# A two-operation token shift, expert dots moved into earlier stages, five value batches a unit, and gathers listed by when their slots come free

## The chip, the cores and the metric

The kernel runs on one core of one Trainium2 chip, in float32. The metric is the device time of one execution in microseconds, the median of the runs. The core's engines are named as the profile names them: PE (TensorE matmuls), PEld (its weight loads), DVE (VectorE), ACT (ScalarE), POOL (GpSimd) and SP (SyncE), with 16 DMA engines beside them.

## The reference, cut to what matters

A first block of two layers works on 256 image tokens `x` and 256 context tokens `xc`; a second block of one hybrid layer follows (the change does not touch it). A layer of the first block has a token mixer and an expert part (PEER):

```
z = h @ w_in
zr = z + mu[0] * (z_previous - z) + mu[1] * (z_next - z)      # token_shift; zero outside
y_a = rwkv(zr)                       # two scans, 16 heads of 64, forward and backward
y_b = conv_branch(z)                 # gated 31-tap depthwise convolution
x = x + gate1 * ((gates_a * y_a + gates_b * y_b) @ w_out)

# peer: for each token, 8 heads x 16 chosen experts out of 16384, 1024 numbers each
act[t, k] = gelu(h[t] . u[eidx[t, k]]) * gw[t, k]
out[t] = sum_k act[t, k] * v[eidx[t, k]]
```

The expert part is applied to `xc` in layer 0, to `x` in layer 0 and to `x` in layer 1. In layer 1 the context tokens only feed the scan states.

## The kernel before, in words

**Stages.** The program is written out by hand as a sequence of stages (`k.stage()`), each with one instruction list for each engine, and a stage starts when the one before it is done. Inside a stage engines wait for one another through counting semaphores. A matrix product is `gemm`: blocks of 128 output channels, weights from a ring of four 512 KB slots that SP fills, PSUM banks 0 to 3 evacuated by ACT. With `shift` given, DVE then does the token shift of each block (lines 226 to 241): a difference of neighbours, two one-column operations for the edges and two scalar_tensor_tensor operations, five in all.

**One expert job.** 256 tokens x 128 experts are fetched as 256 *rows* and 64 *batches*. A row is one indirect DMA from `peer_u` (128 partitions x 4 KB = 512 KB, line 1729) and one *dot* on DVE (128 x 1024, line 1688); rows go through a ring of four slots. A batch is one small POOL copy (line 1745), four indirect DMAs from `peer_v` (line 1751), 512 KB each, into four free slots, and 8 matmuls over the 4 strips (line 1713). The first 32 batches open when 128 dots are done and weighed (`weigh_tile`), the other 32 when 256 dots are done and the first 32 are summed (`finish_tile`).

**Where a job is spread.** Three jobs exist. The context job of layer 0 is spread over the token mixer of `x` in layer 0 and its `choose_experts`; the token job of layer 0 over the context mixer of layer 1, and what is left is done alone in `finish_experts`; the job of layer 1 is done wholly alone. How much a stage takes is written by hand: `use_rows(k, dve, n)` puts n dots at that place of DVE's list, `use_batches(k, pe, n)` n batches at that place of PE's list. `fetch_rows(k, pool)` then writes the gathers for them into POOL's list, each behind a wait for its slot to come free; POOL issues strictly in that order. The slots of values are `spare_slots`: the four weight slots and three borrowed buffers while the eight RWKV units of layer 0 run (seven, so one batch whole and three quarters of the next), four and four buffers in layer 1 and four plus the four of the row ring in `choose_experts`.

**The RWKV unit.** `rwkv_unit` handles a quarter of the heads in one direction; there are eight in a mixer. PE and DVE pass small products back and forth: a start part (pair products), a 14-step inversion (`invert_pairs`, q = 0 to 13), and two scan steps (n = 0, 1). `fetch_rows` is called three times in a unit: after the start part, after the inversion, at the end. While values are open, a unit takes 20 dots (DVE) and 4 batches (PE: one at its start, two in step n = 0, one in step n = 1); while they are not, 27 dots (26 in layer 1).

**`choose_experts`.** PE runs 16 blocks of the query product with 8 batches among them, then the transposes of `h`, then all batches that are left (line 1984), and behind them the transposes of the chosen expert numbers, for which DVE's sort must be done (line 2034).

## Time and profile before

| | us |
|---|---|
| median of 3 runs (lowest, highest) | 5637.92 (5622.06, 5640.57) |
| the profiled execution, its own time | 5637.74 |
| its span | 5636.0 |
| PE busy | 3746.9 |
| DVE busy | 2625.6 |
| POOL busy | 1682.2 |

1.74 us of the profiled execution lie outside its span. All times below are microseconds from the span's start. In a timeline row the columns are start, length, engine, line, operation, output and inputs, count, and in brackets the idle time just before it with what ended it. A row may merge several neighbouring instructions (x16). The mean granted clock of PE was 0.817 over the span.

### The profile page before, as it was taken

What the parts mean: (1) busy time and instruction counts of PE and PEld (TensorE: products, weight loads), DVE (VectorE), ACT (ScalarE), POOL (GpSimd) and SP (SyncE); (2) the same over time, 40 slices, a digit from 0 to 9 for tenths busy, and PEclk for the clock granted to TensorE, in tenths of its full rate; (3) what the DMA queues carried; (4) which work ended last, traced back from release to release, by engine and by line L of the source; (5) the groups of instructions that cost most, each with busy time, mean ns of one, the idle gap of its engine ahead of it and who ended that gap; (6) DMA issues with size and microseconds to landing.
All of it is one profiled execution on the core that took longest, in us unless ns stands there. A gap on an engine that the chain in (4) does not pass through costs nothing. (4 is left out here: it accounts for less than half of the span.)

```text
span 5636.0 us, 92419 instructions
## 1 busy us (share of the span) xinstructions
PE 3746.9 (66%) x37266; PEld 2834.6 (50%) x37266; DVE 2625.6 (47%) x6231; ACT 994.2 (18%) x2532; POOL 1682.2 (30%) x1745
## 2 busy tenths in 40 slices
PE   7888875896666684866625688887400456555988
PEld 5677764785444451655401367776300013554877
DVE  3556536668665261687640024663899101233110
ACT  1123311113222010233300012431100000111110
POOL 0000000325556344355677300000277773000000
PEclk9899987997788885867868899998755788766999
DMA  6520034766778687577899633002499996100433
GB/s 264 189 90 3 3 112 172 291 250 192 238 267 282 238 298 263 185 236 256 282 390 409 244 109 101 3 3 79 150 389 405 405 409 246 60 17 31 142 114 125
DMA packets 299199, 1118.78 MB, mean 199 GB/s; under 512 B 33712, under 2 KB 39104, under 8 KB 290240
## 3 DMA queue, kind: packets, MB, share of 16 engines
q0 software_dynamic: 221184, 805.40, 39.1%
q1 hardware_dynamic: 77632, 307.95, 15.9%
q8 instruction: 279, 4.57, 0.3%
q14 instruction: 104, 0.85, 0.0%
HBM read 1112.18 MB, written 1.05 MB: 198 GB/s over the span
## 5 line engine op out<-in xcount | busy, mean ns | idle before, releaser
L1729 POOL DMA_INDIRECT ring<-in_peer_u,expert_number x617 | 712.9, 1155 | 1812.9 <-DVE expert_number L2026 1173.4
L159 PE MATMUL psum<-h,weight_ring 128*128 128x256 f32 x3904 | 871.9, 387 | 45.8 <-PEq L85 45.8
L1688 DVE CUSTOM_DVE_ANT_0 ring<-ring,tok 128x1024 f32<-128x1024 f32 x617 | 746.1, 1222 | 251.0 <-DMA ring<-in_peer_u,expert_number 227.6
L159 PEld LDWEIGHTS psum<-h,weight_ring 128*128 128x128 f32 x3904 | 759.3, 195 | 157.7 <-issue 48.1
L1713 PE MATMUL psum<-spare,picked 128*32 128x512 f32 x1856 | 322.3, 828 | 437.3 <-DMA spare<-in_peer_v,expert_turned 422.4
L1751 POOL DMA_INDIRECT spare<-in_peer_v,expert_turned x464 | 440.2, 949 | 124.5 <-issue 115.0
L1713 PEld LDWEIGHTS psum<-spare,picked 128*32 128x32 f32 x1856 | 69.9, 133 | 686.2 <-issue 686.2
L1870 DVE SCALAR_TENSOR_TENSOR x_tokens<-psum,gate,x_tokens 128x128 f32<-128x128 f32 x32 | 8.6, 343 | 608.3 <-PE psum L1859 608.3
L1961 PE MATMUL psum<-h,weight_ring 128*128 128x256 f32 x768 | 186.5, 399 | 44.0 <-DMA weight_ring<-in_w_q 29.3
L1377 PE MATMUL psum<-h,weight_ring 128*128 128x256 f32 x768 | 177.9, 394 | 28.2 <-PEq L85 23.6
L1688 DVE CUSTOM_DVE_ANT_0 spare<-spare,tok 128x1024 f32<-128x1024 f32 x151 | 185.0, 1225 | 21.4 <-DMA spare<-in_peer_u,expert_number 15.6
L1961 PEld LDWEIGHTS psum<-h,weight_ring 128*128 128x128 f32 x768 | 150.6, 201 | 73.9 <-DMA weight_ring<-in_w_q 30.2
L1377 PEld LDWEIGHTS psum<-h,weight_ring 128*128 128x128 f32 x768 | 151.4, 199 | 53.3 <-issue 26.3
L1090 POOL MEMSET W<- 128x1024 f32 x4 | 3.8, 953 | 579.5 <-POOLq L85 579.5
L2135 PE MATMUL psum<-constants,dots 128*128 128x128 f32 x3 | 1.4, 475 | 254.7 <-DVE dots L2107 254.7
L1729 POOL DMA_INDIRECT spare<-in_peer_u,expert_number x151 | 155.3, 1029 | 45.7 <-issue 45.7
L1713 PE MATMUL psum<-weight_ring,picked 128*32 128x512 f32 x332 | 84.4, 894 | 108.8 <-DMA weight_ring<-in_peer_v,expert_turned 108.8
L641 ACT ACTIVATE E<-psum 128x256 f32<-128x256 f32 x288 | 110.4, 383 | 259.0 <-PE psum L660 252.3
L1323 DVE SCALAR_TENSOR_TENSOR zc<-u,vec,zc 128x256 f32<-128x256 f32 x336 | 133.3, 479 | 0.0
L1850 ACT ACTIVATE y<-psum 128x512 f32<-128x512 f32 x12 | 6.5, 594 | 709.3 <-PEq L85 709.3
L2135 PEld LDWEIGHTS psum<-constants,dots 128*128 128x128 f32 x3 | 0.5, 183 | 256.9 <-DVE dots L2107 255.2
L185 ACT ACTIVATE z<-psum 128x256 f32 x132 | 50.6, 383 | 436.7 <-PE psum L159 436.7
(552 smaller groups left out, 7133.6 us busy)
## 6 DMA issues: line engine op xcount, KB each, us to landing
weight_ring<-in_w_in SPq DMA_DIRECT2D x228, 512.0 KB, 3.5
ada_ring<-in_ada_w SPq DMA_DIRECT2D x34, 1024.0 KB, 9.2
weight_ring<-in_w_q SPq DMA_DIRECT2D x48, 512.0 KB, 5.0
weight_ring<-in_w_out SPq DMA_DIRECT2D x32, 512.0 KB, 3.6
weight_ring<-in_w_gate SPq DMA_DIRECT2D x32, 512.0 KB, 3.7
weight_ring<-in_w_mlp_in SPq DMA_DIRECT2D x32, 512.0 KB, 3.5
weight_ring<-in_w_mlp_out SPq DMA_DIRECT2D x8, 2048.0 KB, 8.4
ring<-in_ada_w SPq DMA_DIRECT2D x14, 1024.0 KB, 14.7
```

The costliest lines, as they stand in the source:

```text
L159: mm = pe.matmul(k.bank(slot, tokens), ring[:, slot, j * P:j * P + P], rhs(j), start=(j == 0), stop=(j == w.kt - 1))
L185: ins = act.activation(out, product, ACT.Copy)
L641: act.activation(out[:, g], product(q, g), ACT.Copy).then_inc(k.act_step.up(), 1)
L1323: ins = dve.scalar_tensor_tensor(conv[:, j, :], src, w, conv[:, j, :], ALU.mult, ALU.add)
L1377: mm = pe.matmul(k.bank(slot, 256), k.ring[:, slot, j * P:j * P + P], rhs(j), start=(j == 0), stop=(j == 7))
L1688: dve.tensor_tensor_reduce(place.rows, place.rows, b.tok[:, tile, :], 1.0, 0.0, ALU.mult, ALU.add, b.dots[:, tile, slot:slot + 1]).then_in ...
L1713: mm = pe.matmul(out, place.window.columns[:, strip, STRIP - 1 - c:2 * STRIP - 1 - c], part.rows[:, 512 * half:512 * half + 512], start=(c ...
L1729: pool.indirect_dma_start(place.rows, None, b.tables["u"], bass.IndirectOffsetOnAxis(ap=b.number[:, r:r + 1], axis=0)).then_inc(place.sem, 16)
L1751: pool.indirect_dma_start(part.rows, None, b.tables["v"], bass.IndirectOffsetOnAxis(ap=job.lists.turned[:, token:token + 1], axis=0)).then ...
L1850: act.activation(b.y[:, 512 * half:512 * half + 512], k.bank(bank + half), ACT.Copy).then_inc(k.act_step.up(), 1)
L1870: dve.scalar_tensor_tensor(part, k.psum[:, P * j:P * j + P], job.lists.gate[:, j:j + 1], part, ALU.mult, ALU.add).then_inc(k.vec_step.up(), 1)
L1961: mm = pe.matmul(k.bank(slot, 256), k.ring[:, slot, j * P:j * P + P], h[:, j, :], start=(j == 0), stop=(j == 7))
```

## The change

1. **Token shift.** ACT writes each block twice: once unchanged into `unshifted`, once multiplied by `kept` = 1 - mu0 - mu1. DVE adds the two neighbours, two scalar_tensor_tensor operations a block. Two small operations ahead make `kept`, and ACT waits for them.
2. **Dots.** `channel_norm` takes 6 (before 4, or 2 when it centers), `gates_and_taps` 24 (16), the shifted `gemm` 1.5 per block (0.75), `key_norms` 3 and 5 (1 and 2).
3. **Batches.** A unit takes five: at its start, behind q = 3 and q = 8 of the inversion, and one in each scan step; the second one of n = 0 is gone.
4. **Gathers.** One `fetch_rows` a unit, at its end. Every use notes a step (`step_of`: 100 for each stage plus the place in it), slots and windows carry the step at which they came free, and the gathers of a stage are sorted by it, rows before batches at equal steps. Before, rows were dealt evenly between the batches.
5. **`value_slots`** lends the row ring to values only from the stage after the last dot.
6. **`choose_experts`**: the left batches stand behind the transposes of the expert numbers.

```diff
@@ -40,6 +40,7 @@
+        self.stages, self.step = 0, 0
@@ -82,8 +83,14 @@
+        self.stages += 1
+        self.step_of(0)
...
+    def step_of(self, n):
...
+        self.step = 100 * self.stages + n
@@ -121,7 +128,8 @@
-            steps = mem.enter_context(k.sbuf("token_steps", [2, tokens + 1]))
+            unshifted = mem.enter_context(k.sbuf("unshifted", [w.blocks, tokens]))
+            kept = mem.enter_context(k.sbuf("share_kept", [w.blocks]))
@@ -176,12 +184,17 @@
+                if shift is not None:
+                    act.wait_ge(k.vec_step.sem, k.vec_step.at(2))
...
-                        if sigmoid is None:
+                        if shift is not None:
+                            act.activation(unshifted[:, bass.ds(i * SLOTS_W + slot, 1), :], product, ACT.Copy)
+                            ins = act.activation(out, product, ACT.Copy, scale=kept[:, bass.ds(i * SLOTS_W + slot, 1)])
+                        elif sigmoid is None:
@@ -224,28 +237,25 @@
-                        block_n, e = i * SLOTS_W + slot, steps[:, slot % 2, :]
-                        z = dst[:, bass.ds(block_n, 1), :].rearrange("p n t -> p (n t)")
+                        block_n = bass.ds(i * SLOTS_W + slot, 1)
...
-                        dve.tensor_tensor(e[:, 1:tokens], dst[:, bass.ds(block_n, 1), 1:tokens].rearrange("p n t -> p (n t)"),
-                                          dst[:, bass.ds(block_n, 1), 0:tokens - 1].rearrange("p n t -> p (n t)"), ALU.subtract).then_inc(up.sem, 1)
-                        dve.tensor_copy(e[:, 0:1], dst[:, bass.ds(block_n, 1), 0:1].rearrange("p n t -> p (n t)")).then_inc(up.sem, 1)
-                        dve.tensor_scalar(e[:, tokens:tokens + 1], dst[:, bass.ds(block_n, 1), tokens - 1:tokens].rearrange("p n t -> p (n t)"),
-                                          -1.0, None, ALU.mult).then_inc(up.sem, 1)
-                        for n in range(2):
...
-                            dve.wait_ge(up.sem, i * (5 * SLOTS_W) + up.at(5 * slot + 3 + n))
-                            dve.scalar_tensor_tensor(z, e[:, n:n + tokens], shift[:, n, bass.ds(block_n, 1)], z, ALU.mult, ALU.subtract
-                                                     ).then_inc(up.sem, 1)
...
-                    use_rows(k, dve, 3 * w.blocks // 4)
+                        for n, (to, source) in enumerate(((slice(1, tokens), slice(0, tokens - 1)), (slice(0, tokens - 1), slice(1, tokens)))):
+                            if n:
...
+                                dve.wait_ge(up.sem, i * (2 * SLOTS_W) + up.at(2 + 2 * slot + n))
+                            z, neighbour = (t[:, block_n, part].rearrange("p n t -> p (n t)") for t, part in ((dst, to), (unshifted, source)))
+                            dve.scalar_tensor_tensor(z, neighbour, shift[:, n, block_n], z, ALU.mult, ALU.add).then_inc(up.sem, 1)
...
+                    dve.tensor_tensor(kept[:], shift[:, 0], shift[:, 1], ALU.add).then_inc(up.sem, 1)
+                    dve.wait_ge(up.sem, up.at(1))
+                    dve.tensor_scalar(kept[:], kept[:], -1.0, 1.0, ALU.mult, ALU.add).then_inc(up.sem, 1)
+                    use_rows(k, dve, 3 * w.blocks // 2)
...
-                k.vec_step.up(5 * w.blocks)
+                k.vec_step.up(2 + 2 * w.blocks)
@@ -394,7 +404,7 @@
             chain = chained(k, dve)
-            use_rows(k, dve, 2 if center else 4)
+            use_rows(k, dve, 6)
@@ -622,12 +632,9 @@
             unit.between(q, dve)
+            k.step_of(2 + q)
...
                 use_rows(k, dve, 1)
...
-    @block.gpsimd
-    def _(pool):
-        fetch_rows(k, pool)
@@ -659,6 +666,9 @@
+            if q in (3, 8):
+                k.step_of(2 + q)
+                use_batches(k, pe, 1)
@@ -829,6 +839,7 @@
+            k.step_of(0)
@@ -837,10 +848,12 @@
+            k.step_of(1)
...
+            k.step_of(0)
@@ -890,10 +903,6 @@
-        @block.gpsimd
-        def _(pool):
-            fetch_rows(k, pool)
@@ -939,6 +948,7 @@
+            k.step_of(17)
@@ -974,6 +984,7 @@
+                k.step_of(18 + 2 * n)
@@ -989,6 +1000,7 @@
+                k.step_of(22)
@@ -1030,6 +1042,7 @@
+                k.step_of(18 + 2 * n)
@@ -1053,8 +1066,6 @@
-                if n == 0:
-                    use_batches(k, pe, 1)
@@ -1126,14 +1137,14 @@
             chain(dve.reciprocal(norm, norm))
-            use_rows(k, dve, 1)
+            use_rows(k, dve, 3)
...
                 chain(dve.tensor_tensor(part, part, halves[n], ALU.mult))
-            use_rows(k, dve, 2)
+            use_rows(k, dve, 5)
@@ -1406,7 +1417,7 @@
                 conv_taps(k, L, u, conv, reach, taps, True)(dve)
-                use_rows(k, dve, 16)
+                use_rows(k, dve, 24)
@@ -1591,17 +1602,17 @@
-        self.freed, self.taken, self.left = None, False, 0
+        self.freed, self.taken, self.left, self.step = None, False, 0, 0
...
-        return names(rows=self.rows, sem=self.landed.sem, landed=self.landed.count, freed=self.freed, slot=self)
...
-    def leave(self, sem, value, order=0):
-        self.freed, self.taken, self.left = (sem, value), False, order
+        return names(rows=self.rows, sem=self.landed.sem, landed=self.landed.count, freed=self.freed, step=self.step, slot=self)
...
+    def leave(self, sem, value, step, order=0):
+        self.freed, self.taken, self.step, self.left = (sem, value), False, step, order
@@ -1609,7 +1620,7 @@
-        self.columns, self.freed = columns, None
+        self.columns, self.freed, self.step = columns, None, 0
@@ -1618,7 +1629,7 @@
-        self.row, self.fetched, self.places, self.turn = 0, 0, {}, 0
+        self.row, self.fetched, self.places, self.turn, self.stage = 0, 0, {}, 0, 0
@@ -1658,7 +1669,7 @@
-    slots = [*k.spare_slots, *(job.shared.slots[0:4] if job.row == 2 * SLOTS and not k.own_slots else [])]
+    slots = [*k.spare_slots, *(job.shared.slots[0:4] if job.row == 2 * SLOTS and job.stage < k.stages and not k.own_slots else [])]
@@ -1668,7 +1679,7 @@
-                              free=window.freed)
+                              free=window.freed, step=window.step)
@@ -1687,8 +1698,8 @@
-        place.slot.leave(k.row_used.sem, k.row_used.count)
-        job.row = r + 1
+        place.slot.leave(k.row_used.sem, k.row_used.count, k.step)
+        job.row, job.stage = r + 1, k.stages
@@ -1713,9 +1724,9 @@
-        place.window.freed = k.batch_used.sem, k.batch_used.count
+        place.window.freed, place.window.step = (k.batch_used.sem, k.batch_used.count), k.step
...
-            part.slot.leave(k.batch_used.sem, k.batch_used.count, k.batch_used.count)
+            part.slot.leave(k.batch_used.sem, k.batch_used.count, k.step, k.batch_used.count)
@@ -1763,15 +1774,13 @@
-    done = 0
-    for n, m in enumerate(batches):
-        upto = len(rows) * (n + 1) // (len(batches) + 1)
-        for r in rows[done:upto]:
-            gather_row(k, pool, r)
-        done = upto
-        gather_batch(k, pool, m)
-    for r in rows[done:]:
-        gather_row(k, pool, r)
+    wanted = [(place_row(job, r).step, 0, r, gather_row) for r in rows]
+    latest = 0
+    for m in batches:
+        latest = max(latest, place_batch(k, m).step, *(part.step for part in place_batch(k, m).parts))
+        wanted.append((latest, 1, m, gather_batch))
+    for _, _, n, gather in sorted(wanted, key=lambda w: w[:3]):
+        gather(k, pool, n)
@@ -1981,8 +1990,6 @@
-                use_batches(k, pe, 2 * BATCHES)
-                k.spare_slots = []
@@ -2033,6 +2040,8 @@
+                use_batches(k, pe, 2 * BATCHES)
+                k.spare_slots = []
```

## Rows read from the trace of the kernel before

**Rows 1.** The page, busy time by engine over the whole span.
```profile
PE 3746.9 (66%) x37266; PEld 2834.6 (50%) x37266; DVE 2625.6 (47%) x6231; ACT 994.2 (18%) x2532; POOL 1682.2 (30%) x1745
```

**Rows 2.** Busy time by window: length, engines, PE's granted clock, DMA share, GB/s.
```profile
1500.00:1600.00 100.00, 72.62 (x1384) 54.89 (x1381) 63.81 (x129) 30.08 (x81) 60.16 (x57) 0.86 0.82 284
2900.00:3000.00 100.00, 51.21 (x289) 11.02 (x289) 3.34 (x7) 0.59 (x2) 78.74 (x100) 0.77 1.02 406
4200.00:4300.00 100.00, 0.47 (x1) 0.18 (x1) 95.68 (x158) 0.59 (x2) 76.24 (x79) 0.50 1.02 408
```

**Rows 3.** DVE timeline: starts of RWKV units (L826), weighing (L1828), first dot afterwards (L1688).
```profile
1296.37 0.69 DVE L826 TENSOR_TENSOR KR<-kk,E 128x512 f32<-128x512 f32 x1 [0.59 <-PEq L85]
...
1419.20 0.69 DVE L826 TENSOR_TENSOR KR<-kk,E 128x512 f32<-128x512 f32 x1 [1.21 <-PEq L85]
1504.07 0.69 DVE L826 TENSOR_TENSOR KR<-kk,E 128x512 f32<-128x512 f32 x1 [0.40 <-PEq L85]
...
1844.30 0.29 DVE L1828 TENSOR_TENSOR dots<-dots,gw 128x128 f32<-128x128 f32 x1 [2.00 <-ACT dots L1819]
...
2358.42 0.69 DVE L826 TENSOR_TENSOR KR<-kk,E 128x512 f32<-128x512 f32 x1 [0.59 <-PEq L85]
...
2586.54 0.69 DVE L826 TENSOR_TENSOR KR<-kk,E 128x512 f32<-128x512 f32 x1 [0.40 <-PEq L85]
2646.05 0.70 DVE L826 TENSOR_TENSOR KR<-kk,E 128x512 f32<-128x512 f32 x1 [1.21 <-PEq L85]
...
2848.20 1.23 DVE L1688 CUSTOM_DVE_ANT_0 spare<-spare,tok 128x1024 f32<-128x1024 f32 x1 [5.32 <-DMA spare<-in_peer_u,expert_number]
...
3496.19 0.69 DVE L826 TENSOR_TENSOR KR<-kk,E 128x512 f32<-128x512 f32 x1 [0.57 <-PEq L85]
...
3786.70 0.69 DVE L826 TENSOR_TENSOR KR<-kk,E 128x512 f32<-128x512 f32 x1 [0.40 <-PEq L85]
```

**Rows 4.** DVE timeline in the token job's `choose_experts`: end of the sort.
```profile
2117.34 0.29 DVE L2026 TENSOR_SCALAR expert_number<-expert 128x256 uint32<-128x256 f32 x1
```

**Rows 5.** PE timeline there: first, second and last of the 20 batches left.
```profile
2087.29 1.93 PE L1713 MATMUL psum<-ring,picked 128*32 128x512 f32 x16 [1.34 <-DMA ring<-in_peer_v,expert_turned]
2094.20 3.64 PE L1713 MATMUL psum<-more,picked 128*32 128x512 f32 x16 [4.99 <-DMA more<-in_peer_v,expert_turned]
...
2220.65 2.61 PE L1713 MATMUL psum<-more,picked 128*32 128x512 f32 x16 [2.02 <-DMA more<-in_peer_v,expert_turned]
```

**Rows 6.** PE timeline in `finish_experts` of the token job: first and last of 52 batches.
```profile
2907.36 3.64 PE L1713 MATMUL psum<-spare,picked 128*32 128x512 f32 x16 [3.02 <-DMA spare<-in_peer_v,expert_turned]
...
3170.46 3.50 PE L1713 MATMUL psum<-spare,picked 128*32 128x512 f32 x16 [3.10 <-DMA spare<-in_peer_v,expert_turned]
```

**Rows 7.** Groups of instructions by line: count, busy us, mean ns, idle before.
```profile
L1688 DVE CUSTOM_DVE_ANT_0 ring<-ring,tok 128x1024 f32<-128x1024 f32 x617 | 746.1, 1222 | 251.0 <-DMA ring<-in_peer_u,expert_number 227.6 <-PEq L85 11.9 <-DVE E L723 2.2
...
L240 DVE SCALAR_TENSOR_TENSOR z<-token_steps,vec,z 128x256 f32 x208 | 100.8, 484 | 30.2 <-DVE token_steps L235 0.6 <-DVE z L240 0.6
```

**Rows 8.** DVE timeline, layer 0: last gates dot; shifted product's first, last dot, last shift; key norm.
```profile
1107.83 1.23 DVE L1688 CUSTOM_DVE_ANT_0 ring<-ring,tok 128x1024 f32<-128x1024 f32 x1 [0.20 <-DMA ring<-in_peer_u,expert_number]
...
1168.58 1.23 DVE L1688 CUSTOM_DVE_ANT_0 ring<-ring,tok 128x1024 f32<-128x1024 f32 x1 [0.43 <-PEq L85]
...
1212.10 1.23 DVE L1688 CUSTOM_DVE_ANT_0 ring<-ring,tok 128x1024 f32<-128x1024 f32 x1 [1.17 <-DMA ring<-in_peer_u,expert_number]
...
1269.57 1.11 DVE L240 SCALAR_TENSOR_TENSOR z<-token_steps,vec,z 128x256 f32 x2
...
1281.11 1.22 DVE L1688 CUSTOM_DVE_ANT_0 ring<-ring,tok 128x1024 f32<-128x1024 f32 x1
```

**Rows 9.** PE timeline, last part of the gates product in layer 0.
```profile
1099.64 14.19 PE L1377 MATMUL psum<-h,weight_ring 128*128 128x256 f32 x65
```

**Rows 10.** PE timeline inside the unit that starts at 1504.07 (values open).
```profile
1555.14 3.64 PE L1713 MATMUL psum<-weight_ring,picked 128*32 128x512 f32 x16 [13.26 <-DMA weight_ring<-in_peer_v,expert_turned]
```

**Rows 11.** DVE timeline inside the same unit.
```profile
1556.80 1.23 DVE L1688 CUSTOM_DVE_ANT_0 ring<-ring,tok 128x1024 f32<-128x1024 f32 x1 [7.33 <-DMA ring<-in_peer_u,expert_number]
```

## The prediction

> **What bounds the kernel now.** I read the page first: no engine is full, PE is busy 66%, DVE 47%, POOL 30% of the span [rows 1]. An average says nothing here, so next the busy time by windows. Two kinds of stretch stand out. From 2900 to 3000 nothing but gathers of values runs: POOL issues 80 of them (its 100 instructions are those and 20 small copies), the DMA share is 1.02 at 406 GB/s. From 4200 to 4300 it is rows: DVE 96% busy, POOL 76%, DMA 1.02 [rows 2]. There the DMA engines are the bound, at 1.28 us for each 512 KB gather. In a window of RWKV units with values open (1500 to 1600) nobody is at a bound: DMA share 0.82, PE 73%, DVE 64%, POOL 60% [rows 2].
>
> Then the timelines, for where the stages begin. In layer 0 the eight units take 547.9 us: the first two, without values, 61.4 each, the first with values 84.9, the last five (340.2) 68.0 each. In layer 1 four units without values take 57.0 each, the fifth 59.5, and 202.1 us pass from the sixth to the first dot of `finish_experts`. The mixer without a job has units of 41.5 [rows 3]. In `choose_experts` of the image tokens the sort ends at 2117.3 [rows 4], but PE still works on 20 left batches until 2223.3, one in 7.0 us: (2220.65 - 2094.20)/18 [rows 5]. In `finish_experts` one batch takes 5.16 us, (3170.46 - 2907.36)/51, which is 1.29 a gather [rows 6].
>
> So a gather is worth 1.28 to 1.75 us where it stands alone, and the question is what it costs where it is put instead.
>
> **Counting the change.** Going through the calls in order gives, for the context job, dots done ahead of the units: before 4+28+16+2+14+21+3 = 88, after 6+28+24+6+14+42+8 = 128. So the first tile is weighed ahead of unit 0, not of unit 2. Before, units 2 to 7 take 4 batches each and 12 follow up to `choose_experts`: 36, leaving 8 inside its product and 20 behind. After: units 0 to 5 take 20 dots and 5 batches, unit 6 the last 8 dots and 2 batches (the first tile's 32 are then used up), unit 7 no dots and 5 batches, then the same 12: 49, leaving 8 and 7. For the token job in layer 1: before 4+15+3 dots and 26 in each of five units, then three units with 19 dots and 4 batches: left are 47 dots (43 gathers) and 52 batches. After 6+30+8 and 26 in four units, then four with 19 dots and 5 batches: left are 32 dots (28 gathers) and 44 batches.
>
> **Token shift.** On DVE a block falls from five operations to two of 0.48 us [rows 7]: 28 of them end in about 31 us, where 28 old ones took 1213 to 1270.7 [rows 8] (partly waiting for PE). ACT's second activation has cover: PE makes a block in 3.6 us (four of them in the 14.2 of [rows 9]), two activations are under 1 us. Where no job runs, PE sets the pace, so nothing: below 0 by the last block's tail, above 0.4 us, three times.
>
> **Dots put into earlier stages**, layer 0. Beside a product the dots come slowly, because weights share the DMA: 21 dots from 1168.6 to 1213.2 [rows 8], the first four already landed, 17 others 2.27 us apart. A landed dot costs DVE 1.2 [rows 7].
> - Shifted product: 21 more at 2.27 are 48 us, so the dots end at 1261, the 28 shifts at 1292 instead of 1270.7: +21. Bounds: 1.8 a dot gives +11, 2.4 gives +25.
> - Gates: PE ends at 1113.8 [rows 9], the 16th dot at 1109 [rows 8]. Eight more end at 1127 at the slow pace, at 1121 if the weights' traffic stops at 1114. I take +10 (7 to 13).
> - The two norms: +2 dots at 2.3 = +4; +4 dots, two landed, two not: +8 (5 to 10). DVE's next operation there is on the path.
> - Key norm: DVE is the path from 1281 [rows 8]; 5 dots at 1.2 and a wait: +7 (6 to 10).
> Sum +50 (33 to 62). In layer 1: norm +4, shifted product of 20 blocks (15 more dots, 34 us, against about 25 us that the shorter shift and the slack give back) +9, key norm +7: +20 (10 to 27).
>
> The Trainium skill, page "DMA: Bandwidth & Descriptors", section "Anatomy of one DMA", has 2.0 us plus bytes/436e3 for a DMA, an estimate of 3.2 us for 512 KB. Four slots would then turn round in 4.4 us, a dot in 1.1, and the 48 us above would be 25: the sum would be 23 lower. The trace has 2.27 beside weights, and I keep that.
>
> **The unit with values.** No row shows one with five batches in these places. The old unit has avoidable waits: PE sat idle 13.26 us for values whose gathers POOL had put behind others [rows 10], and DVE 7.33 for its row at the same time [rows 11]. Two batches in n = 0 and one in n = 1 stand close together, and with seven slots the fourth gather of a batch waits for the batch before. Afterwards the places are spread about 8 to 15 us apart, each gap with some 4 + 4 gathers. From below, 40 gathers at 1.28 and five copies make 54 us (POOL and DMA bound). From above, the old 68.0 plus one batch at its lone pace of 7.0 makes 75. Between them: PE's own work. 41.5 us without a job [rows 3], 20 dots on a shared chain (27 cost 61.4 - 41.5 = 20 us, so 15), and five batches at 1.93 to 3.64 us, the same 16 matmuls at PE's two clock levels [rows 5], partly in idle time: 7 us of the 10 to 18. I take 64 in layer 0, 62 in layer 1 (19 dots, eight slots). The first unit with values costs 12 more (84.9 against 68.0 before, less what the better order gives). Unit 6 about 50, unit 7 about 52, two weighings and the finishing of a tile 12. The mixed queue matters too: `fetch_rows` now writes one list a unit, so each row gather can stand behind a batch gather that waits for PE; DVE's next dot is behind it, and PE's chain behind that dot.
> - Layer 0: 76 + 5 x 64 + 50 + 52 + 12 = 510 against 547.9: -38, and -4 for the tile finished here and not later: -42 (bounds: units of 54 give -100, of 75 give +20).
> - Layer 1: 4 x 57 + 4 + 74 + 3 x 62 + 8 = 500 against 489.8: +10 (-22 to +55).
>
> **`choose_experts`.** Seven batches are left, but they now stand behind the transposes that need the sort (2117). Two have landed by then (3.6 each), five follow at 7.0 [rows 5]: end near 2163 against 2223.3: -60 (-50 to -70). Had they stayed in front they would have ended near 2136; the move costs some 25 us of what fewer batches gain.
>
> **`finish_experts`.** 15 + 32 = 47 gathers fewer at 1.28: -60 (-56 to -62).
>
> **The sum.** 50 - 42 - 60 + 20 + 10 - 60 = -82, from the profiled execution's 5637.7 (span 5636.0 and 1.7 outside), which is also the median of the runs: 5556 us. One microsecond in the length of a unit with values moves the result by some 10.
>
> **Rivals.** Faster or slower than no change can be told here from about 0.3%, 17 us.
> 1. *The spread works fully*, units near 56: -82 - 80, 5476. For it: POOL's bound of 54. Against: PE's chain. 0.15.
> 2. *The early dots and the units cost more*, units of 68 to 70.5: 5596 to 5621. 0.10; of 70.5 to 74, no difference: 0.10.
> 3. *The single list blocks POOL.* The step numbers of DVE and PE are only guesses of time; POOL stops in front of a batch whose fourth slot PE has not left, rows and dots stop too, and two batches now lie in the inversion, where no other work covers PE's wait. At 3 us for each of five batches units take 75 to 76: 5556 + 110 = 5666, slower. It decides from 70.5 (no gain) and 74 (a loss). For it: the two waits of [rows 10, 11] show such a stop. 0.10.
> 4. *DVE's two-input operations lock POOL out.* 20 dots at 1.2, some 18 us of other two-input work and 40 gathers at 0.98 would add up to 81 us a unit: 5726. In the window 4200 to 4300 DVE is busy 96% and POOL 76% at once [rows 2], so they overlap. 0.03. This is the exclusive lock of the Trainium skill, page "SBUF — State Buffer", section "SBUF: two separate sides"; the trace does not show it for the dots.
>
> The forecast, units of 60 to 68 and a time of 5516 to 5596, has 0.52. Faster is 0.52 + 0.15 + 0.10 = 0.77, same 0.10, slower 0.13. The range reaches into rivals 1 and 2: 5490 to 5635.
>
> **What would show it.** Right: unit starts 60 to 68 us apart with PE waits for values under 5 us each; `finish_experts` of the token job about 60 us shorter with 44 batches at 5.16; seven batches after the sort's end. Wrong: gaps over 70 between unit starts, POOL idle before L1751 or L1729 waiting for PE, DVE idle for rows; the shifted product of layer 0 ending under 10 or over 25 us later within its stage; or a clock of PE that falls in the units.

## The result, and the profile after

The changed kernel takes 5648.5 us (median of 20 runs; the kernel before 5633.0 in its 20 beside them): ratio 1.0028, 95% interval 1.0015 to 1.0041. The interval does not reach 1, so the kernel is a little slower, but by less than the 0.3% set above as the least that can be told from no change. It is 92 us above the forecast of 5556, and above the upper end of the range, 5635. The profiled execution takes 5645.9 us, span 5644.1, against 5636.0 before.

The page's busy times, and the busy time by window (length, PE, PEld, DVE, ACT, POOL, PE's granted clock, DMA share, GB/s), kernel after:
```profile
PE 3681.7 (65%) x37266; PEld 2806.6 (50%) x37266; DVE 2575.0 (46%) x5927; ACT 1033.7 (18%) x2636; POOL 1680.2 (30%) x1745
```
```profile
1600.00:1700.00 100.00, 68.20 (x1190) 46.98 (x1192) 54.22 (x110) 23.82 (x64) 53.64 (x57) 0.82 0.75 254
4200.00:4300.00 100.00, 0.47 (x1) 0.18 (x1) 93.97 (x154) 0.59 (x2) 76.82 (x77) 0.50 1.02 400
```
In the units with values PE, DVE, POOL and DMA are all *less* busy than in [rows 2] (POOL 54 against 60, DMA share 0.75 against 0.82), although more work was put there. Nothing filled up; everybody waits. Where rows alone are fetched little changed (400 GB/s against 408).

DVE timeline, kernel after: first weighing, unit starts (L836), weighing and tile update, unit 7, first operation behind the units, sort, layer 1:
```profile
1341.61 0.29 DVE L1837 TENSOR_TENSOR dots<-dots,gw 128x128 f32<-128x128 f32 x1 [2.18 <-ACT dots L1828]
...
1432.84 0.69 DVE L836 TENSOR_TENSOR KR<-kk,E 128x512 f32<-128x512 f32 x1 [0.40 <-PEq L88]
...
1838.97 0.69 DVE L836 TENSOR_TENSOR KR<-kk,E 128x512 f32<-128x512 f32 x1 [0.40 <-PEq L88]
...
1950.70 2.29 DVE L1224 TENSOR_REDUCE row<-o 128x32 f32<-128x2048 f32 x1 [0.39 <-PEq L88]
...
2218.11 0.29 DVE L2033 TENSOR_SCALAR expert_number<-expert 128x256 uint32<-128x256 f32 x1
...
2420.93 0.69 DVE L836 TENSOR_TENSOR KR<-kk,E 128x512 f32<-128x512 f32 x1 [0.60 <-PEq L88]
...
2719.03 0.69 DVE L836 TENSOR_TENSOR KR<-kk,E 128x512 f32<-128x512 f32 x1 [0.40 <-PEq L88]
2780.85 0.76 DVE L836 TENSOR_TENSOR KR<-kk,E 128x512 f32<-128x512 f32 x1 [0.40 <-PEq L88]
2841.41 0.77 DVE L836 TENSOR_TENSOR KR<-kk,E 128x512 f32<-128x512 f32 x1 [0.40 <-PEq L88]
...
2911.29 1.23 DVE L1699 CUSTOM_DVE_ANT_0 spare<-spare,tok 128x1024 f32<-128x1024 f32 x1 [2.23 <-DMA spare<-in_peer_u,expert_number]
```
Five units with values in layer 0 take (1838.97 - 1432.84)/5 = 81.2 us each, against 70.2 (four of them, 1504.07 to 1784.7) in the kernel before, and the layer's units 609.1 (1341.61 to 1950.70) against 547.9 of [rows 3]. In layer 1 a unit with values takes 61.2 (2719.03 to 2841.41, two of them).

PE timeline, kernel after: batches behind the sort (first and last of seven), then `finish_experts` of the token job (first and last but one of 44 batches):
```profile
2218.75 3.64 PE L1724 MATMUL psum<-ring,picked 128*32 128x512 f32 x16
...
2260.70 3.65 PE L1724 MATMUL psum<-ring,picked 128*32 128x512 f32 x16 [6.53 <-DMA ring<-in_peer_v,expert_turned]
...
2953.26 3.64 PE L1724 MATMUL psum<-spare,picked 128*32 128x512 f32 x16 [3.48 <-DMA spare<-in_peer_v,expert_turned]
...
3170.00 3.29 PE L1724 MATMUL psum<-spare,picked 128*32 128x512 f32 x16 [3.15 <-DMA spare<-in_peer_v,expert_turned]
```
From the sort to the end of the last batch are 46.2 us, against 105.9 in [rows 4, 5]. From the first dot of `finish_experts` to its tile update are 267.4 us (2911.29 to 3178.70), against 327.5 before (2848.20 to 3175.73).

What a unit of 81 us looks like: POOL's timeline in the unit that starts at 1595.99, then PE's batches there (start, duration, what, idle before and its releaser), kernel after:
```profile
1633.00 0.94 POOL L1762 DMA_INDIRECT weight_ring<-in_peer_v,expert_turned  x1 [2.90 <-PE psum L1724]
1634.25 0.94 POOL L1740 DMA_INDIRECT ring<-in_peer_u,expert_number  x1 [0.30 <-issue]
1641.40 0.94 POOL L1740 DMA_INDIRECT ring<-in_peer_u,expert_number  x1 [6.21 <-DVE dots L1699]
1644.55 1.68 POOL L1740 DMA_INDIRECT ring<-in_peer_u,expert_number  x1 [2.21 <-DVE dots L1699]
1646.54 0.94 POOL L1740 DMA_INDIRECT ring<-in_peer_u,expert_number  x1 [0.30 <-issue]
1649.93 1.68 POOL L1740 DMA_INDIRECT ring<-in_peer_u,expert_number  x1 [2.45 <-DVE dots L1699]
1651.92 1.03 POOL L1740 DMA_INDIRECT ring<-in_peer_u,expert_number  x1 [0.30 <-issue]
1654.86 1.68 POOL L1740 DMA_INDIRECT ring<-in_peer_u,expert_number  x1 [1.91 <-DVE dots L1699]
1656.84 1.61 POOL L1740 DMA_INDIRECT ring<-in_peer_u,expert_number  x1 [0.30 <-issue]
1658.46 0.38 POOL L1756 COPY picked<-weights 128x4 f32<-128x4 f32 x1
1658.99 1.24 POOL L1762 DMA_INDIRECT x_tokens<-in_peer_v,expert_turned  x1 [0.15 <-issue]
```
```profile
1631.60 1.09 PE L1724 MATMUL psum<-x_tokens,picked 128*32 128x512 f32 x2
...
1645.54 1.92 PE L1724 MATMUL psum<-weight_ring,picked 128*32 128x512 f32 x16
...
1669.70 1.07 PE L1724 MATMUL psum<-x_tokens,picked 128*32 128x512 f32 x2 [9.89 <-DMA weight_ring<-in_peer_v,expert_turned]
```
Layer 0 has seven value slots, of which two lie in `x_tokens`, one in `y`, four in the weight ring. PE leaves the first three at 1632.7; the fourth that the next batch needs is one that PE leaves at 1647.5. `fetch_rows` lists the whole batch by the latest of the four, so all four gathers stand behind every row of a lower step. POOL waits 6.21 + 2.21 + 2.45 + 1.91 = 12.8 us for DVE's dots with three value slots empty, starts on them at 1658.99, and PE then waits 9.89. POOL stops in front of a batch's fourth slot too, but for less: 2.90 us at 1633.00. Over the five middle units it waits 23.7 us a unit in front of rows (18.3 in the four of the kernel before) and 3.0 in front of batches (2.2).

### The profile page after: what moved, and what is told of

Read it like the earlier page. It is cut to its first block and busy times, and to the rows that moved or that the text cites. A ratio compares the mean times of both kernels' runs of the same rounds, so it can differ in the third digit from the quotient of the medians.

```text
span 5644.1 us, 92050 instructions
## 1 busy us (share of the span) xinstructions
PE 3681.7 (65%) x37266; PEld 2806.6 (50%) x37266; DVE 2575.0 (46%) x5927; ACT 1033.7 (18%) x2636; POOL 1680.2 (30%) x1745
## 5 line engine op out<-in xcount | busy, mean ns | idle before, releaser
L1740 POOL DMA_INDIRECT ring<-in_peer_u,expert_number x624 | 705.7, 1131 | 1814.6 <-DVE expert_number L2033 1170.3
L1724 PE MATMUL psum<-spare,picked 128*32 128x512 f32 x1728 | 288.5, 801 | 428.5 <-DMA spare<-in_peer_v,expert_turned 262.1
L1762 POOL DMA_INDIRECT spare<-in_peer_v,expert_turned x432 | 410.9, 951 | 115.8 <-issue 109.2
L1724 PE MATMUL psum<-weight_ring,picked 128*32 128x512 f32 x512 | 121.6, 809 | 93.8 <-DMA weight_ring<-in_peer_v,expert_turned 66.5
L248 DVE SCALAR_TENSOR_TENSOR z<-unshifted,vec,z x208 | 97.5, 483 | 157.1 <-ACT z L196 135.5
L631 DVE TENSOR_TENSOR TT<-psum,TT 128x256 f32<-128x256 f32 x192 | 79.8, 423 | 193.3 <-PE psum L667 190.8
L1740 POOL DMA_INDIRECT spare<-in_peer_u,expert_number x144 | 153.1, 1063 | 43.6 <-issue 43.6
L1762 POOL DMA_INDIRECT weight_ring<-in_peer_v,expert_turned x128 | 136.9, 1070 | 53.3 <-issue 32.0
```

Source lines behind the costliest of these rows:

```text
L248: dve.scalar_tensor_tensor(z, neighbour, shift[:, n, block_n], z, ALU.mult, ALU.add).then_inc(up.sem, 1)
L631: ins = dve.tensor_tensor(out[:, g], product(q, g), added[:, g], ALU.add)
L1724: mm = pe.matmul(out, place.window.columns[:, strip, STRIP - 1 - c:2 * STRIP - 1 - c], part.rows[:, 512 * half:512 * half + 512], start=(c ...
L1740: pool.indirect_dma_start(place.rows, None, b.tables["u"], bass.IndirectOffsetOnAxis(ap=b.number[:, r:r + 1], axis=0)).then_inc(place.sem, 16)
L1762: pool.indirect_dma_start(part.rows, None, b.tables["v"], bass.IndirectOffsetOnAxis(ap=job.lists.turned[:, token:token + 1], axis=0)).then ...
```

## The experiments

The kernels ran in five groups of three or four, one chip to a group. In three groups gathers were slower for every kernel: back to back 376 GB/s in e8_shift_only (347 to 382 in windows of the others), where [rows 2] have 408. The kernel before has a median of 5828, 5826 and 5815 us there, so each ratio is to the kernel before of the same group. "Unit" is the mean of the middle units with values in layer 0 (four or five of them), with PE's wait for values and DVE's for rows in such a unit.

| kernel | batches a unit | ratio to before, interval | unit, us | PE waits | DVE waits |
|---|---|---|---|---|---|
| before | 4 | 1 | 70.2 | 19 | 8 |
| e9_after_again (unaltered) | 5 | 1.0029, 1.0011 to 1.0047 | 80.7 | 22 | 0 |
| e10_parts_again | 5 | 0.9927, 0.9900 to 0.9955 | 69.9 | 12 | 2 |
| e11_parts_old_counts | 5 | 0.9896, 0.9870 to 0.9922 | 70.4 | 12 | 2 |
| e12_parts_old_places | 4 | 1.0072, 1.0047 to 1.0097 | 74.5 | 23 | 3 |
| slower gathers: e8_shift_only | 4 | 1.0012, 0.9998 to 1.0026 | 80.5 | 16 | 7 |
| e5_front | 5 | 1.0097, 1.0072 to 1.0122 | 91.0 | 16 | 0 |
| e6_early_old | 5 | 1.0101, 1.0081 to 1.0121 | 92.6 | 14 | 0 |
| e7_parts_front | 5 | 1.0046, 1.0027 to 1.0066 | 87.1 | 9 | 0 |
| e13_values_first | 5 | 1.0015, 0.9998 to 1.0032 | 87.4 | 0 | 7 |
| e14_four_spread | 4 | 1.0016, 0.9998 to 1.0035 | 79.2 | 0 | 1 |
| e15_three_lists | 4 | 1.0049, 1.0030 to 1.0067 | 81.3 | 19 | 2 |
| e16_best_again | 5 | 1.0001, 0.9982 to 1.0019 | 85.1 | 10 | 0 |
| e17_one_list_again | 4 | 1.0092, 1.0063 to 1.0121 | 85.4 | 19 | 0 |
| e18_three_again | 4 | 1.0043, 1.0027 to 1.0060 | 80.9 | 20 | 2 |

**Seven slots in layer 1 too.** The four kernels of the first group (this one, e2_parts_apart, e3_four_places and e4_dealt) were run once each, beside one run of the kernel before at 5632.8 us, so they have no interval; what is read from them are the units.
```diff
-            hosts = spare_rows(k, 8, *(more[:, j, :] for j in range(4)))
+            hosts = spare_rows(k, 8, *(more[:, j, :] for j in range(3)))
```


> Base is the changed kernel; in layer 1 the units get seven slots for values instead of eight (three borrowed buffers, not four). In the changed kernel the units with values are 81.5 us apart in layer 0 (seven slots, PE waiting about 22 us a unit for values) and 61 in layer 1 (eight slots, 6.5). Theory A, with seven slots a batch's last slot is released by the batch just before it, so the whole batch sorts late in POOL's list: the second and third layer-1 unit go from 61.8 and 60.6 to 76 to 82 us, PE's wait for values in them from 6.5 to some 20. Theory B, the two batches inside the inversion and the extra Y work of layer 0 make the long unit: layer 1 stays at 61 within 2.

5739.8 us. Layer 1's units with values rise from 69.0, 61.8 and 60.6 us to 86.8, 78.8 and 80.5, PE's waits in each from 12.4, 6.6 and 6.4 to 27.9, 23.1 and 23.5. PE timeline of this kernel in layer 1: where the fourth slot is the ring's, the batch waits, which is the shape of the unit above.
```profile
2740.59 1.07 PE L1724 MATMUL psum<-more,picked 128*32 128x512 f32 x3 [10.01 <-DMA weight_ring<-in_peer_v,expert_turned]
```
Seven slots are enough to make units of 80 us out of units of 62. Gathers were not slower there: `finish_experts`, right behind these units, takes 268.1 us, against 267.4.

**Each gather by its own slot.** Only the listing changes; the four gathers keep their order.
```diff
-        latest = max(latest, place_batch(k, m).step, *(part.step for part in place_batch(k, m).parts))
-        wanted.append((latest, 1, m, gather_batch))
+        place = place_batch(k, m)
+        latest = max(latest, place.step)
+        wanted.append((latest, 1, (STRIPS + 1) * m, pick_batch))
+        for strip, part in enumerate(place.parts):
+            wanted.append((max(latest, part.step), 1, (STRIPS + 1) * m + strip + 1, gather_part))
```


> Base is the changed kernel; each of a batch's four gathers is listed by the step at which its own slot came free, not all four by the latest; seven slots stay. Theory A: three of four gathers go out one batch earlier, only the fourth is late; the steady layer-0 units go from 81.5 to 66 to 73 us and PE's wait from 22 to about 8. Theory B (places of the batches): 78 or more. Layer 1, where all four slots come free together, stays at 61.

5599.6 us, with units of 69.4. The same kernel again, beside the unaltered changed kernel:

> The changed kernel once more, unaltered, beside the others of this group. On a chip with 1.28 us a gather: 1.0028 of the kernel before. Where a gather is slower (1.40 us, 376 GB/s instead of 408, as the four runs before this group had it), the units with values should suffer more in it than in the kernel before (five batches and a late fourth gather): about 1.012 to 1.015, with units of 90 us.

> The changed kernel with each of a batch's four gathers listed by its own slot's step (the kernel of e2_parts_apart). Theory A (the list by the latest slot): 25 to 50 us under the changed kernel of this group on any chip; ratio to before about 0.994 with gathers at 1.28 us, 1.005 at 1.40. Theory B (the places of the batches): within 10 us of the changed kernel.

5592.1 us, ratio 0.9927, where the changed kernel has 1.0029. Listing a batch by its latest slot costs 57 us, 11 in each of five units: more than the 25 to 50 expected, though PE's wait fell only to 12 us and not to 8. The POOL and PE timelines of e10_parts_again at the place of the stall above:
```profile
1556.47 1.35 POOL L1766 DMA_INDIRECT x_tokens<-in_peer_v,expert_turned  x1 [0.16 <-issue]
1558.13 0.94 POOL L1766 DMA_INDIRECT x_tokens<-in_peer_v,expert_turned  x1 [0.30 <-issue]
1559.38 0.94 POOL L1766 DMA_INDIRECT y<-in_peer_v,expert_turned  x1 [0.30 <-issue]
```
```profile
1560.18 3.64 PE L1724 MATMUL psum<-weight_ring,picked 128*32 128x512 f32 x16 [4.94 <-DMA weight_ring<-in_peer_v,expert_turned]
1572.53 1.07 PE L1724 MATMUL psum<-x_tokens,picked 128*32 128x512 f32 x2 [5.62 <-DMA weight_ring<-in_peer_v,expert_turned]
```
The three gathers now go out before PE reaches the batch that frees the fourth slot. POOL's waits in front of rows fall to 14.6 us a unit. One rival is PE's clock: does it fall and make PE's own work longer? One middle unit by window, kernel after and then e10_parts_again (columns as in [rows 2]):
```profile
1595.99:1677.56 81.57, 50.30 (x840) 34.23 (x840) 43.65 (x88) 19.37 (x54) 44.84 (x45) 0.79 0.75 257
```
```profile
1569.53:1638.73 69.20, 47.78 (x840) 33.93 (x840) 43.87 (x88) 19.26 (x54) 46.46 (x46) 0.84 0.87 305
```
Over the five middle units PE's mean granted clock is 0.79 in the kernel after and 0.82 in e10_parts_again, and PE is busy 50.1 and 48.6 us a unit with the same matmuls. So 1.5 of the 11 us is longer work of PE, and its waits for values (22 us against 12) are the rest.

On slower gathers the same edit is worth less: e5_front and e7_parts_front, described below, differ in it alone and were run in one group. They have ratios of 1.0097 and 1.0046, 26 us apart, and units of 91.0 and 87.1. What the expectation of e9_after_again says of slower gathers was not tested, since gathers moved at 408 GB/s in its group.

**Back to the old places.**
```diff
-            if q in (3, 8):
-                k.step_of(2 + q)
-                use_batches(k, pe, 1)
...
+                if n == 0:
+                    use_batches(k, pe, 1)
```


> Base is the changed kernel; the batches of a unit stand where they stood before (start, two in step n = 0, one in n = 1: four, not five), all else as changed. Theory A: the lateness comes from the list, so units with values in layer 0 stay above the old 68.0, at 70 to 76, with PE waits of 18 or more. Theory B: they fall to 62 to 68. In both the batches left in choose_experts of the image tokens grow from 7 to about 13 behind its product.

5720.7 us, units of 79.2 with only four batches and 29 us of waits: the late list makes units long at these places too, by more than the 70 to 76 expected.

> Base is the changed kernel; the one list a unit is kept, but rows are dealt evenly between its batches as before, instead of the sort by step. Theory A: a batch no longer waits in the list for all rows of lower step, PE's wait of 22 us a unit in layer 0 falls to 8 to 15 and the units from 81.5 to 68 to 75, perhaps with DVE waits for rows (0 in the changed kernel) of 5 to 10. Theory B: 80 or more.

5800.9 us, units of 91.7. Here my expectation missed: rows and batches dealt evenly, as before, but in one list a unit, makes the slowest kernel of the first two groups. Sorting by steps is not the mistake; the number of lists was not in my theory. The next kernel has the list by parts at the old places, again with one list a unit:

> As e11_parts_old_counts, but the batches at the four places of the kernel before (start, two in the first half of the state pass, one in the second): only the list differs from the kernel before, and the token shift. Theory A says that a list by steps with the parts apart beats the old dealing of rows and batches: units of 62 to 66 us in layer 0 against its 70, ratio 0.990 to 0.996. Theory B says that the five places gain by themselves: then this one is no better than the kernel before and e11_parts_old_counts is well under it. e3_four_places (the same places with whole batches, 5721) bears on neither, since its list was late.

1.0072: the theory that the list alone beats the old dealing fell, and theory B stands (e11_parts_old_counts, which differs in the places and the fifth batch alone, has 0.9896 in the same group). Next comes the same kernel with `fetch_rows` called at three points of a unit. It was run on slower gathers and has 1.0049, which fits neither of its two expectations, so both kernels were then run in one group:

> As e12_parts_old_places (1.0072), but with three lists in a unit, where the kernel before has them, in place of one. If one list a unit is what made e12_parts_old_places slow (batches are listed only as far as slots are known to come free, and with one list all is decided at once): units of 66 to 70 and 0.990 to 0.997. If the old places are the cause: units stay at 74 and 1.007.

> The kernel of e12_parts_old_places: old places, one list a unit. 1.007 in a group like its first; if one list is what costs, 0.4 to 0.8% over e18_three_again.

> The kernel of e15_three_lists: old places, three lists a unit. If the number of lists matters: under e17_one_list_again by 0.4 to 0.8%, near the kernel before. If it does not: within 0.2% of e17_one_list_again.

In one group: 1.0092 with one list, 1.0043 with three, units of 85.4 and 80.9. At the old places one list costs 0.5% on slower gathers. Even with three lists the order by steps does not beat the kernel before there (e8_shift_only in its own such group: 1.0012, units of 80.5). So the gain of e10_parts_again needs both, the spread places and the list by parts; either alone loses: the kernel after has the first alone, e12_parts_old_places the second.

**What holds such a unit at 70.** Both kernels were run on slower gathers only.

> As e11_parts_old_counts (0.9896), but where a gather of values and one of a row fall on the same step, the values go first. If the list's order is what makes PE wait (12 us a unit): units of 64 to 67 and a time 20 to 40 us under e11_parts_old_counts. If the DMA engines are the bound (share 0.86 in its units): PE's wait turns into DVE's for rows and the unit stays at 70.

> As e11_parts_old_counts, without the fifth batch of a unit (the one in the second half of the state pass): four batches at the unit's start, after two steps of the inversion, and in the first half of the state pass. If the fifth batch costs what a gather's time says (4 at 1.28 = 5.1 us and a copy), units are 64 to 65 and the seven batches more that are left cost 7 us each where they stand: no difference in the whole. If it costs 10 or more: units of 58 to 60 and a gain of 20 us. If it is hidden: units stay at 70 and the time rises by 40.

Groups of instructions inside one unit (count, busy us, mean ns, idle before), e7_parts_front and then e13_values_first:
```profile
L1699 DVE CUSTOM_DVE_ANT_0 ring<-ring,tok 128x1024 f32<-128x1024 f32 x20 | 23.8, 1219 | 0.3 <-DVE E L733 0.3
...
L1724 PE MATMUL psum<-weight_ring,picked 128*32 128x512 f32 x56 | 13.9, 863 | 8.2 <-DMA weight_ring<-in_peer_v,expert_turned 8.1
```
```profile
L1699 DVE CUSTOM_DVE_ANT_0 ring<-ring,tok 128x1024 f32<-128x1024 f32 x20 | 23.9, 1218 | 7.5 <-DMA ring<-in_peer_u,expert_number 7.1 <-DVE E L733 0.3
...
L1724 PE MATMUL psum<-weight_ring,picked 128*32 128x512 f32 x56 | 13.0, 862 | 6.4 <-PEq L88 6.4
```
Values first: no wait of PE is put down to values any more, DVE waits 7 us for rows instead, and the unit stays at 87. But the test took away less than it seems to. PE still stands idle 6.4 us before the first batch of the unit, now until its own sequencer starts (PEq), where in e7_parts_front it stood 3.2 us for values at that place. All its idle time before batches fell from 9 us to 7. With four batches at spread places the unit is 79.2 against 85.1 to 87.4 with five: a fifth batch costs 6 to 8 us in a unit (8.2 within the group), about what one costs behind the units, and the whole does not move (1.0015 and 1.0016). I expected 5, or over 10. This points to the spread, and not the fifth batch, as what counts: with four batches and one list a unit the spread places have 1.0016, the old ones 1.0092 (e17_one_list_again, another group). What holds the unit at 70 where gathers run at 408 GB/s was not tried.

**The early dots and the left batches.**
```diff
-            use_rows(k, dve, 6)
+            use_rows(k, dve, 2 if center else 4)
```


> The counts of dots in the early stages (norms, gates, shifted product, key norm) are those of the kernel before; units, list and token shift stay changed. The early stages should give back 50 us in layer 0 and 25 in layer 1. The 40 dots then belong to the units again. If a dot costs as much in a unit as in an early stage (2.3 us), the time is the same. If units with values are slow because of values and not of dots, the first two units carry the dots without a batch (61 us instead of 80) and 10 batches move to choose_experts at 7 us each: 5648 - 50 - 40 + 70 - 20 in layer 1, some 5610. If the list by the latest slot is the cause that I take it for, the slow units stay at 80 us and unit 6 rises from 52 to 80.

> The seven left batches of the context's choose_experts are put back in front of the transposes that need the sort, as in the kernel before; all else is the changed kernel. If the prediction's reading holds, PE has idle time for them while the sort runs, and the stretch from the sort's end to the update in finish_tile falls from 48 us to some 23 (time about 5623 against 5648). The rival: the batches' gathers, at 1.3 us each, and their matmuls at the low clock lie in the way of PE's scores, which the sort waits for; then the sort ends later by what is saved behind it, and the time stays at 5640 to 5650.

Both in a group of slower gathers: 1.0101 (1.0081 to 1.0121) and 1.0097 (1.0072 to 1.0122). The changed kernel itself was not in it, so only their stretches are read. That e6_early_old is as fast as e5_front, which gains the 30 us below, suggests that giving the early dots back is worth about as much; this is argued, not shown. In e5_front the stretch from the first operation behind the units to the sort takes 266.7 us (267.4 in the kernel after, with gathers at 408 GB/s), and from the sort to the tile update 18.2 instead of 48.0. The last two batches, PE timeline of e5_front; the sort ended at 2300.4:
```profile
2306.18 3.64 PE L1724 MATMUL psum<-more,picked 128*32 128x512 f32 x16 [5.40 <-DMA more<-in_peer_v,expert_turned]
2312.12 3.62 PE L1724 MATMUL psum<-ring,picked 128*32 128x512 f32 x16 [2.30 <-DMA ring<-in_peer_v,expert_turned]
```
The sort is not delayed; moving the batches behind it costs some 30 us (I had written 25).

> The four gathers of a batch listed each by its own slot's step (as in e2_parts_apart, 5600) together with the left batches in front of the sort's transposes (e5_front). If the two gains add: 5600 - 25 = 5575. If the front place only delays the sort: 5600. Units as in e2_parts_apart, about 70 us in layer 0.

1.0046 on slower gathers, no test of 5575.

> The list by each slot's own step, the counts of dots in the early stages as in the kernel before, the left batches in front of the sort's transposes; values at the new five places. If the early dots, at 2.3 us each, were the bad half of the change: 50 + 25 us back for two units more without values, ten batches more at 5 to 7 us and some ten more in layer 1's end: 10 to 30 us under e10_parts_again. If they were worth it: the same or above.

5576.8 us, ratio 0.9896, the fastest of all, 15 us under e10_parts_again, inside the expected 10 to 30. From the sort to the first unit layer 0 takes 322 us instead of 383. Against that, 34 batches instead of 27 stand behind its units and cost 27 us more up to the last of them, even though they are back in front, and `finish_experts` of the token job takes 313.3 us instead of 268.7. This kernel changes two things at once, and the front place alone was worth some 30 us in e5_front, so the 15 us do not show that giving the early dots back gains anything where gathers run at 408 GB/s. The pair that differs in the early dots alone, e7_parts_front and e16_best_again, was run on slower gathers in two groups: 1.0046 with them, 1.0001 without. There they are not worth what they cost.

> The kernel of e11_parts_old_counts once more. In a group where the kernel before takes 5630: 0.990 again. In one where it takes 5826: 1.0015, as e13_values_first there, if the order at equal steps only moves a wait from PE to DVE; 1.005 or more if that order is worth something.

On slower gathers 1.0001: the best version gains 1.0% where a gather takes 1.28 us and nothing where it takes 1.40. Against e13_values_first (1.0015, another group) the order at equal steps makes no difference that can be told.

**The token shift alone.**

> The kernel before with the token shift's two operations alone. The prediction: where no job runs PE sets the pace, so nothing; where a job runs (28 blocks, 20 blocks) the shift on DVE is shorter by 25 to 30 us, of which part is waiting for PE. 5633 less 0 to 25: I expect 5615 to 5633. The rival: the second activation of ACT delays PE's banks and it costs 0.4 us or more a product: 5633 to 5640.

1.0012, interval 0.9998 to 1.0026: nothing that can be told, as predicted; the 0 to 25 us less that I expected before the run did not come. The stretch of the shifted product of layer 0 takes 105.0 us, against 105.2 in the kernel before.

## Why the prediction was wrong, step by step

- **Early dots, layer 0 (+50).** From the sort of the context job to the first unit: 330.7 before, 380.6 after (to the weighing at 1341.61): +49.9. The shifted product gave +18.7 (said +21), the gates with the norm behind them +21.8 (said +18), the key norm +10 (said +7), the norm ahead of the convolution +2.4 (said +4), the convolution -3 (said 0). The price of a dot beside weights held: 2.23 us measured, where I wrote 2.27 (17 dots in some 40 us of [rows 8] are rather 2.35). By the estimate from the Trainium skill's fit (page "DMA: Bandwidth & Descriptors", section "Anatomy of one DMA") the product's +21 would have been -2; the trace disagrees with it here (+18.7).
- **"I take 64 in layer 0": the step that failed.** 81.2 was measured, 17 too much in five units, and 89.7 instead of 76 in the first: the layer's units took 61 us more than before, where I had 38 less. That is the whole miss of 92 us. The term left out a cost of the list. With seven slots the four gathers of a batch, listed by the latest slot, stand behind rows. Shown by e2 and e10: 11 of the 17 come from this. The other 6, e10's 69.9 against my 64, stay open: e10 still has 12 us of waits for values in a unit, and no run at 408 GB/s tells whether my 15 us for dots, my 7 us for batches or these waits were too little. On slower gathers a fifth batch alone makes a unit 6 to 8 us longer (e14), where my sum had 7 us for all five: that points to the price of the batches, and does not show it. The upper bound of 75 stood too low already: its 68.0 is a mean that takes in the last unit, of 59.6 us, which has 14 dots instead of 20. The four middle units take 70.2, and with a batch 77.2. It also held no price for a longer wait.
- **Rival 3** named the place (the fourth slot of seven, a single list) and the direction, at 0.10, with units of 75 to 76. It was the right mechanism, with two corrections. First, POOL stops mainly in front of *rows*, behind which the batch stands in the list (23.7 us a unit, against 3.0 in front of batches). Second, what it stood on was too low. Its 5666 adds 11 us a unit, and the list cost just that; but it adds them to 64 and not to 70. (3 us for each of five batches, as I wrote, would be 15 and not 11.) PE waited 19 us a unit for values before the change, 22 after it, and 12 with the list mended. I had read both the seven slots and the sort by latest step in the code and had put no price on either in the forecast.
- **One microsecond a unit, 10 us in the result.** This rule took layers 0 and 1 together. By it units of 81 would have given some 5728. Only the five of layer 0 grew, since layer 1 has eight slots, so the time is 5648.5. That it came out near that of the kernel before is a sum of +61 and other steps that cancel, and no sign that the change does little.
- **Layer 1 (+20, +10, -60).** Early stages +21.4 (2264.4 to 2420.93 = 156.6, against 135.2); units 490.4 (2420.93 to 2911.29) against 489.8, +0.6, with 61.2 us where I had 62; `finish_experts` -60.1. Eight slots in place of seven make this difference, as e1 shows.
- **`choose_experts` (-60, and -4 for the tile finished earlier).** 105.9 to 46.2: -59.7; the stretch ahead of the sort 273.0 to 267.4: -5.6. The 25 us lost by the move were 30. All these steps add up to +7.7, with -4.7 ahead of the context's first sort and +5.1 behind the token job: +8.1, the difference of the spans.
- **Token shift (0).** Shown by e8: 1.0012, with an interval that reaches 1, so an effect under 0.26% (15 us) is not excluded.
- **Rivals 1, 2 and 4.** Units of 56 with values, or of 68 to 74 in the middle of layer 0 of the changed kernel, were not seen. Rival 2's "no difference" came true by another way. DVE did not lock POOL out: in the window at 4200 DVE is busy 94% and POOL 77% together.
- **The signs of being wrong** did show: unit starts over 70 us apart, POOL waiting in front of L1740 (rows) and L1762 (values), and a granted clock of 0.79 over the middle units, where it was 0.82 before.

## What to carry to other kernels

When transfers of two kinds share one in-order queue, sort them each by the moment at which their own buffer comes free; a group listed by its latest member holds empty buffers behind work that waits for another engine. Here it cost 11 us in a unit with seven buffers and nothing that shows with eight. Before a group is put into a list, count slots against the size of the group: with seven slots for fours, each group needs one slot that the group just before it leaves. And a gain in evenness (five places) can be lost in the order of the list: change one, look at the waits of both consumers, and only then change the other.

## What the runs showed of the hardware

Gathers back to back ran at 408 GB/s in some groups and at 376 in others, the kernel before included, once on a chip where an earlier group had had 408. Busy time by window in such a group, e8_shift_only, where only rows are fetched:
```profile
4250.00:4350.00 100.00, 0.00 (x0) 0.00 (x0) 88.84 (x145) 0.00 (x0) 76.33 (x73) 0.50 0.99 376
```
The 8% in the gather became 3.2 to 3.5% of the kernel before, and not evenly: units without values took 56 to 65 us in both kinds, those with four batches 80 instead of 70, those with five 87 instead of 70. PE did not wait longer for values in them (9 to 10 us against 12); it was busy longer with the same matmuls, 57.4 us a unit in e7_parts_front against 48.6 in e10_parts_again, at a mean granted clock of 0.78 instead of 0.82. Not all matmuls were slower: the 64x128 ones of L903 took 427 and 379 ns in two units against 278, while the 64x64 ones of L667 that multiply `E` with `E` took 222 in both kinds. What ties this to the gathers was not tried.

Gathers can also be slower in a part of one execution. The second tile of the last job, from its first weighing to its second, took 160.7 us in the kernel before and 174.5 and 171.5 in e1_seven_layer1 and e2_parts_apart, whose earlier `finish_experts` ran at full speed (268.1 and 268.0 us). The times of these two single runs carry that.
